# Low part of every second weight slot summed by DMA in the down projection of the two middle FFN groups

## What is computed

```python
x = x + rms_norm(mixed, g_mix_post)
f = jnp.square(jax.nn.relu(rms_norm(x, g_ffn_pre) @ w_up)) @ w_down
return x + rms_norm(f, g_ffn_post)
```

## Time and profile before

| what | value |
|---|---|
| median of 3 runs | 2080.79 us |
| span of the profiled execution | 2081.2 us (its own time: no separate number is given for what lies around the span) |
| TensorE matmuls | 2046.5 us busy, 98% |
| TensorE weight loads | 1695.0 us, 81% |
| VectorE | 1088.2 us, 52% |
| ScalarE | 998.6 us, 48% |
| GpSimd | 212.1 us, 10% |
| DMA engines, mean busy share | 56%, 183 GB/s |
| mean granted TensorE clock | 0.996 |

### The profile page before, as it was taken

The page is one execution under the profiler, slowest core; times in us unless marked ns, Lnnn a source line. Parts: engine busy times, 40 slices in busy tenths (PEclk is TensorE's granted clock), DMA queues, the critical chain, the costliest instruction groups (busy, mean ns, idle before and its releaser), DMA issues.

```text
span 2081.2 us, 28816 instructions
## 1 busy us (share of the span) xinstructions
PE 2046.5 (98%) x9298; PEld 1695.0 (81%) x9298; DVE 1088.2 (52%) x1105; ACT 998.6 (48%) x1247; POOL 212.1 (10%) x248
## 2 busy tenths in 40 slices
PE   7999999999999999999989999999999999999998
PEld 5888887888888888888878888878888888888886
DVE  6554657554554554554554446664454454454454
ACT  5444656543553453454454446565345444444542
POOL 3951014000000000000120010230000000000001
PEclk9999999999999999999999999999999999999999
DMA  6664454565565555655556544555565566466463
GB/s 214 222 207 137 140 184 160 177 205 186 181 196 188 187 189 188 213 191 182 165 195 208 191 142 130 166 185 183 185 202 191 173 202 200 162 195 230 161 196 128
DMA packets 196518, 381.65 MB, mean 183 GB/s; under 512 B 11904, under 2 KB 14048, under 8 KB 195808
## 3 DMA queue, kind: packets, MB, share of 16 engines
q1 hardware_dynamic: 195776, 379.12, 55.7%
q10 hardware_dynamic: 672, 1.61, 0.2%
HBM read 378.59 MB, written 2.10 MB: 183 GB/s over the span
## 4 chain that ended last, share of the span: by engine, by line
PE 48%; issue 41%; POOL 8%; DMA 1%; DVE 0%; POOLq 0%; ACT 0%; SPq 0%; ACTq 0%; DVEq 0%
PE acc_bank L377 16%; PE acc_bank L379 16%; PE acc_bank L378 16%; POOL acc L1324 2%; POOL h_lo L1297 1%; PE t_bank L637 1%; POOL f_lo L1297 1%; DMA post_row<-in_g_ffn_post 1%; DMA x<-in_x 1%; POOL rstd L1316 0%; PE t_bank L405 0%; POOL band L1453 0%; POOL band L1447 0%; POOL tmp L1417 0%; POOL tmp L1423 0%
## 5 line engine op out<-in xcount | busy, mean ns | idle before, releaser
L964 DVE TENSOR_TENSOR w_lo<-raw,w_hi 128x1024 fp32r<-128x1024 f32 x704 | 871.5, 1250 | 573.4 <-ACT w_hi L692 538.9
L692 ACT CAST w_hi<-raw 128x1024 fp32r<-128x1024 f32 x704 | 734.1, 1052 | 481.7 <-PE acc_bank L379 265.9
L377 PE MATMUL acc_bank<-w_hi,h_hi 128*128 128x512 f32 x1536 | 608.9, 396 | 3.9 <-POOL h_lo L1297 2.2
L379 PE MATMUL acc_bank<-w_hi,h_lo 128*128 128x512 f32 x1536 | 600.0, 391 | 0.0
L378 PE MATMUL acc_bank<-w_lo,h_hi 128*128 128x512 f32 x1536 | 599.3, 390 | 0.0
L377 PE MATMUL acc_bank<-w_hi,f_hi 128*128 128x512 f32 x1216 | 477.4, 393 | 0.0
L379 PE MATMUL acc_bank<-w_hi,f_lo 128*128 128x512 f32 x1216 | 473.5, 389 | 0.0
L378 PE MATMUL acc_bank<-w_lo,f_hi 128*128 128x512 f32 x1216 | 473.1, 389 | 0.0
L377 PEld LDWEIGHTS acc_bank<-w_hi,h_hi 128*128 128x128 f32 x1536 | 289.8, 189 | 65.4 <-DVE w_lo L964 4.0
L379 PEld LDWEIGHTS acc_bank<-w_hi,h_lo 128*128 128x128 f32 x1536 | 289.0, 188 | 61.3
L378 PEld LDWEIGHTS acc_bank<-w_lo,h_hi 128*128 128x128 f32 x1536 | 289.7, 189 | 57.9
(11 more groups left out here) (150 smaller groups left out, 822.2 us busy)
## 6 DMA issues: line engine op xcount, KB each, us to landing
raw<-in_w_up SPq DMA_DIRECT2D x256, 512.0 KB, 4.4
raw<-in_w_down SPq DMA_DIRECT2D x256, 512.0 KB, 5.4
raw<-in_w_in SPq DMA_DIRECT2D x128, 512.0 KB, 4.8
raw<-in_w_out SPq DMA_DIRECT2D x64, 512.0 KB, 5.3
w_pool_s<-in_w_pool SPq DMA_DIRECT2D x2, 1024.0 KB, 8.5
post_row<-in_g_mix_post SPq DMA_DIRECT2D x2, 1024.0 KB, 7.3
post_row<-in_g_ffn_post SPq DMA_DIRECT2D x2, 1024.0 KB, 7.9
out<-x SPq DMA_DIRECT2D x8, 256.0 KB, 2.7
```

The costliest lines, as they stand in the source:

```text
L377: pe.matmul(bank[:, :], xh, wh, start=begin and k == 0, stop=False)
L379: mm = pe.matmul(bank[:, :], xl, wh, start=False, stop=end and k == 1)
L692: act.copy(w_hi[:, half * PAIRS + p, :], raw[:, p, :]).then_inc(hi_made, 1)
L964: dve.tensor_tensor(w_lo[:, slot, :], raw[:, p, :], w_hi[:, slot, :].bitcast(F32), ALU.subtract).then_inc(lo_made, 1)
```

## The change

For the units c = 1 to 3 of the groups 1 and 2 in both layers, the slots with odd p (s1, s3, s1', s3') get their low part in another way. ScalarE makes `w_hi` as before and then writes -`raw`, rounded to F32R, to `w_lo`: the negated high part. That increments `neg_made`. VectorE no longer subtracts for this slot; it waits for `neg_made`, copies one column from `ones` to a new tile `seen`, and this increments `lo_made`, so that the counters stay as they were. GpSimd waits for `neg_made` and issues a DMA that adds the same 512 KB of w_down from HBM onto `w_lo` (`accum_op=ALU.add`), which increments one of four semaphores `lo_landed`. TensorE waits for that semaphore ahead of the pair with t = 0. The load into `raw` stays. These are 2 layers x 2 groups x 3 units x 4 slots = 48 slots of 704.

The weights of unit c + 1 are made while unit c runs, so ScalarE and VectorE do the new work in the loop over c = 0 to 2, and the last turn of the old loop of four (the next group's first unit, split as before) is written out behind it.

```diff
+    def summed_unit(l, g, c):
+
+        return (l * (FF_GROUPS - 2) + g - 1) * (CHUNKS - 1) + c - 1
...
+            def lo_by_dma(l, g, c):
+
+                def before(n, p):
+                    if n < 2 and p % 2:
+                        pe.wait_ge(lo_landed[2 * n + p // 2], 16 * summed_unit(l, g, c) + 16)
+                return before
...
-                        unit(hu + 2 * CHUNKS + c * 2, r + CHUNKS + c, f_hi, f_lo)
+                        unit(hu + 2 * CHUNKS + c * 2, r + CHUNKS + c, f_hi, f_lo,
+                             None if first or last else lo_by_dma(l, g, c))
...
+            def split_hi_neg(hu, half):
+
+                for p in range(PAIRS):
+                    split_hi(hu, half, (p,))
+                    if p % 2:
+                        act.mul(w_lo[:, half * PAIRS + p, :], raw[:, p, :], -1.0
+                                ).then_inc(neg_made, 1)
...
-                        with act.Fori(0, CHUNKS) as c:
-                            split_hi(hu + 8 + c * 2 + 2, 0)
-                            split_hi(hu + 8 + c * 2 + 3, 1)
+                        split = split_hi if first else split_hi_neg
+                        with act.Fori(0, CHUNKS - 1) as c:
+                            split(hu + 8 + c * 2 + 2, 0)
+                            split(hu + 8 + c * 2 + 3, 1)
+                        split_hi(hu + HU_GROUP, 0)
+                        split_hi(hu + HU_GROUP + 1, 1)
...
+            def split_lo_even(l, g, c, hu, half):
+
+                for p in range(PAIRS):
+                    if p % 2 == 0:
+                        split_lo(hu, half, (p,))
+                    else:
+
+                        dve.wait_ge(neg_made, 4 * summed_unit(l, g, c) + 2 * half + p // 2 + 1)
+                        dve.tensor_copy(seen[:, 2 * half + p // 2:2 * half + p // 2 + 1], ones[:, :]).then_inc(lo_made, 1)
...
+            def add_low_parts(l):
+
+                for g in range(1, FF_GROUPS - 1):
+                    for c in range(1, CHUNKS):
+                        for half in range(2):
+                            for p in (1, 3):
+                                k = 2 * half + p // 2
+                                row = g * D + half * HALF_W + p * 2 * P
+                                pool.wait_ge(neg_made, 4 * summed_unit(l, g, c) + k + 1)
+                                src = w_down[l, row:row + 2 * P, c_cols(c)]
+                                pool.dma_start(
+                                    w_lo[:, half * PAIRS + p, :].rearrange("p (k c) -> p k c", k=2),
+                                    src.rearrange("(k p) c -> p k c", p=P),
+                                    accum_op=ALU.add).then_inc(lo_landed[k], 16)
...
+                with pool.If(l < 1):
+                    add_low_parts(0)
+                with pool.If(l > 0):
+                    add_low_parts(1)
```

More of the change, by code:

```diff
@@ L215, in build @@
     warm = own("warm", [P, 1])
+    seen = own("seen", [P, 4])
     rt = [own(f"rt{n}", [P, T, ROPE // 2]) for n in range(6)]
@@ L265, in build @@
     ssa_done = sem("ssa_done")
+    neg_made = sem("neg_made")
+    lo_landed = [sem(f"lo_landed{n}") for n in range(4)]
     def h_cols(t):
@@ L1252, in group @@
                         up_unit(u, False)
-                    with dve.Fori(0, CHUNKS - 1 if last else CHUNKS) as c:
+                    with dve.Fori(0, CHUNKS - 1) as c:
                         down_sum(g, c, 0, first)
-                        split_lo(hu + 8 + c * 2 + 2, 0)
-                        split_lo(hu + 8 + c * 2 + 3, 1)
+                        if first or last:
+                            split_lo(hu + 8 + c * 2 + 2, 0)
+                            split_lo(hu + 8 + c * 2 + 3, 1)
+                        else:
+                            split_lo_even(l, g, c + 1, hu + 8 + c * 2 + 2, 0)
+                            split_lo_even(l, g, c + 1, hu + 8 + c * 2 + 3, 1)
                         down_sum(g, c, 1, first)
                     if not last:
+                        down_sum(g, CHUNKS - 1, 0, first)
+                        split_lo(hu + HU_GROUP, 0)
+                        split_lo(hu + HU_GROUP + 1, 1)
+                        down_sum(g, CHUNKS - 1, 1, first)
                         return
```

## The result

| | median | verdict |
|---|---|---|
| before | 2081.39 us (4 runs) | |
| changed | 2263.99 us (2261.58 to 2270.95, 4 runs) | 1.088 times as long, 95% interval 1.087 to 1.089 |

The change costs 183 us, where 92 were forecast: slower, as predicted, but twice as much and above the range (2250). The profiled execution has a span of 2269.2 us, 188.0 more than before.

What follows compares the result with a forecast made beforehand. TensorE's matmuls were taken to bound the kernel; the 2081.2 us span plus 92 us of waits for adds (12 units of 7.7 us), all else 0, gave 2173 us, range 2115 to 2250.

Steps and rivals of the forecast that it cites:

- What bounds the kernel: Whole kernel: TensorE's matmuls fill 98% of the 2081.2 us span; work taken off VectorE gains nothing.
- the parts costed at nothing: Summed units: 48 subtractions removed from VectorE (60 us busy) and 48 negations of 1.05 us on ScalarE cost 0.
- The adding DMAs' price: DMA engines, four adds per unit: 1.68 to 3.36 us each, the upper taken because an add also reads its destination.
- The chain of s3': Second half: load, copy, negation, issue, landing end at 659.0 against 651.3 wanted; 7.7 us in 12 units, 92 us.
- covered: Rival, 7%: adds fit the engines' spare share, land at 651.0 just before 651.3, TensorE never waits: 2081 us.
- GpSimd has nothing else to do: GpSimd's queue in the changed groups: busy 0.00, so nothing else there holds up the adds; no cost.
- TensorE's clock: After waits: 1.6 us lost behind a 4.61 us standstill; nothing for the point, up to 20 us at the upper end.
- cut in two: TensorE's wait per unit split into about 5 and 3 us, so no clock loss was taken for the point.
- adds much slower: Rival, 15%: issue 1.75 us or more, load 5.8 us late, 12.7 us per unit, plus 20 for the clock: 2253 us.
- the signs named: If right: 12 to 24 TensorE waits of 3 to 8 us, units of 29 to 30 us, adds landing in 6 to 9.

Runs made afterwards that it cites:

- the larger room: The changed kernel with dynamic_dma_scratch_size 2048 in place of 1024, the work the same: 2227.03 us, ratio 1.070.
- s1 stands alone: The changed kernel with room 2048 and only s1 summed by DMA, one add per unit, other slots split as before: 2110.93 us, ratio 1.013.

## Why the prediction was wrong in size

**What bounds the kernel, and the parts costed at nothing.** Right. The negations and the shorter VectorE cost 0 (2081.90 us), and the stages looked at are unchanged: before 397 us and from there to 575 us TensorE is busy 380.60 and 178.00 us, against 380.46 and 178.00.

**The adding DMAs' price.** Nearly right: 3.17 us for 3.36 assumed. Issue 1.22 us for 1.0. Issue and landing together 6.3 us (median) in the changed kernel, 9.1 with the larger room and 8.9 where s1 stands alone, for 8.2 assumed.

**The chain of s3'.** Right in kind, and its total in part by luck. It predicted 92 us of waiting. In the kernel in which adds may overlap, which is the one that this step described, TensorE waits 98.3 us, and in six of the 12 units the longest wait, 4.8 to 6.6 us, is that for s3'. One unit of it:

```profile
644.34 1.05 ACT L707 CAST w_hi<-raw 128x1024 fp32r<-128x1024 f32 x1 [14.23 <-PE acc_bank L386]
663.09 1.05 ACT L707 CAST w_hi<-raw 128x1024 fp32r<-128x1024 f32 x1 [2.62 <-DMA raw<-in_w_down]
...
673.39 0.79 PE L384 MATMUL acc_bank<-w_hi,f_hi 128*128 128x512 f32 x1 [5.38 <-DMA w_lo<-in_w_down]
```

The copy of s3' starts 18.75 us behind that of s0, before it was 12.47: its load is 6.3 us late, where 4.0 was taken. Issue and landing took 7.8 us (665.56 to 673.39) for 8.2. The four waits of this unit are 9.2 us for 7.7 forecast; the mean of the 12 units is 8.2. The place of the waits was off too: I had them at s1' and s3', they come at all four slots (46 of 48). The prediction's own terms say so for s1, and I never added them up: negated at 635.7, 1.0 and 7.2 us more is 643.9, wanted at 643.1. The rival *covered* fails by the single add: 11.05 us against 9.52.

**The step that failed first: "GpSimd has nothing else to do".** It has to wait for its own previous add. In the changed kernel only one fits into the room of 1024, so the four adds of a unit stand in a row; the first three of the unit shown took 8.9, 7.2 and 5.7 us from issue to landing, and the second to the fourth were issued when the one before had landed. No row of before could show it, but the number 1024 stood in the launch code, and its effect deserved a rival. Measured by taking it away: 37 us.

**The step that failed second, and the larger one: TensorE's clock,** taken as nothing, at most 20 us. Measured as growth of busy time: 64.0 us in the changed kernel, 37.5 with more room, 5.3 and 3.1 us per unit. I had sized it by one gap of 4.61 us and the 4 us behind it, 1.6 us lost. Per wait that was about right, since 64.0 over 48 waits is 1.3 us; but I allowed for one such loss in a unit at most, and there are four waits in each. Here half clock lasted from about 643 to 649 us after a wait of 3.20 us, with other waits just before; a wait "cut in two" did not protect it. The length of the last wait alone doesn't settle it: in the next unit the clock fell to 0.50 (664 to 666 us) after a wait of 1.86 us, the only one in 18 us, and stayed at 1.00 (682 to 688 us) after one of 3.05 us.

In the forecast's own terms, on the profiled executions: waits 92 us forecast, 98.3 without the queue and 123.8 with it; clock 0 forecast, 37.5 and 64.0. These two executions lie 52 us apart, the medians 37, so the queue's share in each term is rough.

The runs as a ladder, each step on top of the one before: 0 for the negations, 32 when the adds' traffic is there, 113 more when TensorE waits for the landings, clock included, 37 when the adds queue: 182 us. The steps are not prices that could be added in another order. The forecast's range would have held the kernel with more room (2227), not this one. The rival *adds much slower* came nearer with 2253, but by terms that didn't hold: it had the issue at 1.75 us or more (1.22 measured) and the landing at 9.6 after it (6.3 with the issue), and no queue. Of the signs named, the waits at the high-by-high matmul came, but 48 of 2.6 us in the mean for 12 to 24 of 3 to 8, and a unit took 37.4 us (21.76 + 188.0 / 12) for 29 to 30.

## What to carry to other kernels

Replacing a step that nobody waits for by a DMA in the chain that refills a buffer trades 1.25 us of covered work for 9 us from issue to landing. Compare the time from "free" to "wanted" with issue plus landing before anything else, and take the landing among the loads that run at that moment, not by the unit's mean DMA share. Where GpSimd issues large DMAs, check how many fit into the room that the launch code gives them: a wait of kind "issue" whose end follows the previous landing by some 0.2 us is the sign. And cost every new wait on TensorE with the half clock behind it, wait by wait; here it added about half of the waiting again (64.0 us on 123.8), with the larger room 0.38 of it (37.5 on 98.3).

## What the runs showed of the hardware

- A 512 KB add from GpSimd costs the DMA engines 3.0 to 3.2 us and GpSimd 1.22 us; a copy of the same shape 1.76 and 0.72 us; a load from SyncE about 1.6 us.
- With `dynamic_dma_scratch_size` at 1024 one such add is in flight, or three of half its size, or at least two copies; at 2048 no add had to wait for room, with three in flight (issued at 648.12, 650.97 and 655.85, the first waited for until 656.85).
- From issue to landing an add took 6.3 us (median; 5.6 at the least) when one ran at a time, the last two of a unit beside few loads or none; 9.1 when adds overlapped among loads; and 8.9 for a single add among loads. The long landings go with loads in flight; that adds slow one another beyond that is not shown.
- Waits of TensorE brought its granted clock to 0.50 for several us, once after a single one of 1.86 us: in the changed kernel 48 waits, 123.8 us in all, came with 64.0 us more of busy time.
- With the DMA engines full (share 1.04 in the profile) the core moved 266 GB/s in a stretch of 22 us with the adds' traffic, against 184 to 192 GB/s in the down units before.
